# A sliding-window attention's value products regrouped: one run of sixteen for a pair of heads instead of two of twelve

## What is computed

```python
s = jnp.einsum('bnqhgd,bnjhd->bhgnqj', q, kb).astype(jnp.float32)   # banded: 3 key blocks of 128 for a query block
s = jnp.where(mask, s + bias, lowest)
m = jnp.maximum(jnp.max(s, axis=-1, keepdims=True), sink)
p = jnp.exp(s - m)
p = p / (jnp.sum(p, axis=-1, keepdims=True) + jnp.exp(sink - m))
o = jnp.einsum('bhgnqj,bnjhd->bnqhgd', p.astype(v.dtype), vb).reshape(B, S, D)
return jnp.einsum('bsd,de->bse', o, w_o)
```

## Time and profile before

| | before |
|---|---|
| time, median of 3 executions | 1100.08 us (1099.56 to 1100.72) |
| the profiled execution | 1099.98 us, span 1098.3 us |
| tensor engine busy | 1085.3 us, 99% of the span |
| weight loads busy | 957.7 us, 87% |
| vector engine busy | 879.1 us, 80% |
| scalar engine busy | 597.8 us, 54% |
| granted clock of the tensor engine | 0.998 |

### The profile page before, as it was taken

The page is one execution under the profiler, slowest core; times in us unless marked ns, Lnnn a source line. Parts: engine busy times, 40 slices in busy tenths (PEclk is TensorE's granted clock), DMA queues, the critical chain, the costliest instruction groups (busy, mean ns, idle before and its releaser), DMA issues. The chain is left out here.

```text
span 1098.3 us, 18147 instructions
## 1 busy us (share of the span) xinstructions
PE 1085.3 (99%) x6526; PEld 957.7 (87%) x6526; DVE 879.1 (80%) x1523; ACT 597.8 (54%) x1025; POOL 142.6 (13%) x252
## 2 busy tenths in 40 slices
PE   8999999999999999999999999999999999999997
PEld 6888888888998898898997888888899899899896
DVE  7777888678877876886996799976895895985997
ACT  6777777655425434433554788854542542632544
POOL 6554332100000000000030244200000000000000
PEclk9999999999999999999999999999999999999999
DMA  5422332233323323323242133334313323223312
GB/s 206 124 86 88 90 99 61 84 97 142 116 81 104 104 81 113 99 89 121 78 126 76 54 97 90 88 106 134 101 74 124 91 93 116 96 96 116 118 56 77
DMA packets 37081, 109.64 MB, mean 100 GB/s; under 512 B 6464, under 2 KB 10848, under 8 KB 37008
## 3 DMA queue, kind: packets, MB, share of 16 engines
q1 hardware_dynamic: 32096, 100.74, 27.9%
q0 software_dynamic: 4768, 7.90, 3.0%
q10 hardware_dynamic: 144, 0.02, 0.0%
HBM read 105.93 MB, written 2.70 MB: 99 GB/s over the span
## 5 line engine op out<-in xcount | busy, mean ns | idle before, releaser
L639 PE MATMUL acc<-h_hi,w_parts 128*128 128x512 f32 x736 | 291.0, 395 | 2.6 <-DVE h_lo L1590 1.6
L641 PE MATMUL acc<-h_hi,w_parts 128*128 128x512 f32 x736 | 286.8, 390 | 0.0
L640 PE MATMUL acc<-h_lo,w_parts 128*128 128x512 f32 x736 | 286.6, 389 | 0.0
L639 PEld LDWEIGHTS acc<-h_hi,w_parts 128*128 128x128 f32 x736 | 138.2, 188 | 32.8 <-issue 3.0
L641 PEld LDWEIGHTS acc<-h_hi,w_parts 128*128 128x128 f32 x736 | 138.2, 188 | 29.5
L640 PEld LDWEIGHTS acc<-h_lo,w_parts 128*128 128x128 f32 x736 | 138.3, 188 | 27.8 <-issue 0.5
L1272 ACT CAST w_parts<-w_raw 128x1024 fp32r<-128x1024 f32 x62 | 65.4, 1054 | 131.7 <-PE acc L641 107.5
L639 PE MATMUL pt_ps<-u_hi,w_parts 128*128 128x256 f32 x384 | 109.2, 284 | 0.3 <-DVE x_res L1815 0.2
L640 PE MATMUL pt_ps<-u_lo,w_parts 128*128 128x256 f32 x384 | 108.7, 283 | 0.0
L641 PE MATMUL pt_ps<-u_hi,w_parts 128*128 128x256 f32 x384 | 108.7, 283 | 0.0
L639 PE MATMUL s_ps<-u_hi,w_parts 128*128 128x256 f32 (+1 forms) x292 | 86.5, 296 | 0.0
(11 more groups left out here) (208 smaller groups left out, 2491.2 us busy)
## 6 DMA issues: line engine op xcount, KB each, us to landing
w_raw<-in_wstream SPq DMA_DIRECT2D x148, 512.0 KB, 3.6
d_raw<-in_wstream SPq DMA_DIRECT2D x32, 512.0 KB, 5.2
room<-rpb_reversed POOLq DMA_DIRECT2D x64, 62.0 KB, 2.5
room<-t_shifted POOLq DMA_DIRECT2D x64, 48.0 KB, 2.2
x_res<-in_xT SPq DMA_DIRECT2D x8, 256.0 KB, 6.1
room<-inverse_sums SPq DMA_DIRECT2D x16, 128.0 KB, 3.1
out_y<-x_res SPq DMA_DIRECT2D x8, 256.0 KB, 2.3
inverse_sums<-sw_turned SPq DMA_DIRECT2D x32, 1.0 KB
```

The lines of the kernel that those rows point to most:

```text
L639: nc.tensor.matmul(dst, a[0], b[0], start=start, stop=False, skip_group_check=resumed)
L640: nc.tensor.matmul(dst, a[0], b[1], start=False, stop=False, skip_group_check=resumed)
L641: return nc.tensor.matmul(dst, a[1], b[0], start=False, stop=stop, skip_group_check=resumed)
```

## The change

The turned probabilities get a new layout. The high parts of a pair lie in one room and the low parts in the other. In each the ten combinations of key block and unit stand in the order of the blocks, and within a block in the order of the units, so that all units that see a block are neighbours. A head gets a bank of om_ps for itself, all four query blocks in it. The value products of a pair are now one run: for each head key block 0 (units 0 and 1, 256 columns), block 3 (units 2 and 3, 256 columns), block 1 (units 0 to 2, 384 columns) and block 2 (units 1 to 3, 384 columns), each with the high and the low part, sixteen products with the same 5120 columns in all. The run of the pair before stands between dense_part(1) and the transposes of unit 0. The two old places are empty. After the last step the whole run of the last pair stands where its second group did. sw_o_shift and sw_o_sum read the new banks, and the count of pv_done goes up once a pair instead of twice.

```diff
-        sw_pt = [t.rearrange("p (t b h u q) -> p t b h u q", t=2, b=3, h=2, u=2)
-                 for t in (flat(pt_room),)]
-        sw_pt.insert(0, w_parts[:, 0, :, 2 * CHUNK:].rearrange("p t (b h u q) -> p t b h u q", b=3, h=2, u=2))
+        sw_pt = [w_parts[:, 0, :, 2 * CHUNK:2 * CHUNK + 10 * P].rearrange("p h (c q) -> p c h q", q=P),
+                 flat(pt_room)[:, 0:20 * P].rearrange("p (h c q) -> p c h q", h=2, q=P)]
...
-        sw_near = om_ps[:].rearrange("p g (h u) q -> p g h (u q)", h=2)
+        sw_near = om_ps[:].rearrange("p h n q -> p h (n q)")
...
             first, blocks = SW_BLOCKS[n]
-            first -= n // 2
-            return sw_pt[n // 2][:, t, first:first + blocks, :, n % 2, :].rearrange("p b h q -> p (b h) q")
+            at = 2 * first + n
+            return sw_pt[t][:, at:at + 2 * blocks - 1:2, :, :]
...
-            def sw_values(p, g):
-
-                pe.wait_ge(pt_split, (sw_unit(p, 2 * g + 1) + 1).v)
+            def sw_values(p):
+
+                pe.wait_ge(pt_split, (sw_unit(p, 3) + 1).v)
                 pe.wait_ge(o_summed, (p + HEADS).v)
-                dst = flat(sw_bank(g)).rearrange("p (h u q) -> p h u q", h=2, u=2)
-                both, only = ((0, 1), 2) if g == 0 else ((1, 2), 0)
-
-                def products(hh, b, units, start=False, stop=False):
-                    stationary = flat(v_parts[:, 4 * p.odd + g + b, hh, :, :])
-                    for t in range(2):
-                        ins = nc.tensor.matmul(dst[:, hh, units, :], stationary, sw_pt[g][:, t, b, hh, units, :],
-                                               start=start and t == 0, stop=stop and t == 1)
-                    return ins
-
                 for hh in range(2):
-                    products(hh, both[0], slice(0, 2), start=hh == 0)
-                    products(hh, both[1], slice(0, 2))
-                for hh in range(2):
-                    ins = products(hh, only, slice(1 - g, 2 - g), stop=hh == 1)
+                    for b in (0, 3, 1, 2):
+                        units = [n for n in range(QT) if SW_BLOCKS[n][0] <= b < sum(SW_BLOCKS[n])]
+                        at, count = 2 * b + units[0], len(units)
+                        for t in range(2):
+                            ins = nc.tensor.matmul(om_ps[:, hh, units[0]:units[0] + count, :], flat(v_parts[:, 4 * p.odd + b, hh, :, :]),
+                                                   sw_pt[t][:, at:at + count, hh, :], start=b == 0 and t == 0,
+                                                   stop=b == 2 and t == 1)
                 ins.then_inc(pv_done, 1)
...
                 dense_part(1)
+                if before:
+                    sw_values(p + -1)
                 sw_transpose(p, 0)
-                if before:
-                    sw_values(p + -1, 1)
                 sw_scores(p, 2)
...
                 sw_transpose(p, 2)
-                sw_values(p, 0)
                 dense_part(6)
...
             early_part(CH_SWO, GR_SWO, HEADS, 14, 17)
-            sw_values(At(7), 1)
+            sw_values(At(7))
...
-                act.wait_ge(pv_done, (p * 2 + (UNITS_NA + 2)).v)
+                act.wait_ge(pv_done, (p + (UNITS_NA + 1)).v)
                 act.wait_ge(o_summed, (p + HEADS).v)
-                nc.scalar.copy(by_group(sw_far)[TOP, :, :], sw_near[BOTTOM, :, 0, :])
-                nc.scalar.copy(by_group(sw_far)[BOTTOM, :, :], sw_near[TOP, :, 1, :]).then_inc(o_shifted, 1)
+                nc.scalar.copy(sw_far[TOP, :], sw_near[BOTTOM, 0, :])
+                nc.scalar.copy(sw_far[BOTTOM, :], sw_near[TOP, 1, :]).then_inc(o_shifted, 1)
```

More of the change, by code:

```diff
@@ L378, in sw_pt_part, with by_block @@
             first, blocks = SW_BLOCKS[n]
-            first -= n // 2
-            return sw_pt[n // 2][:, t, first:first + blocks, :, n % 2, :].rearrange("p b h q -> p (b h) q")
-        def sw_bank(g):
-            return misc_ps if g else o_ps
+            at = 2 * first + n
+            return sw_pt[t][:, at:at + 2 * blocks - 1:2, :, :]
+        def by_block(n):
+            return pt_ps[:, 0:2 * SW_BLOCKS[n][1], :].rearrange("p (b h) q -> p b h q", h=2)
         def sw_unit(p, n):
@@ L1395, in sw_pt_high @@
                 act.wait_ge(pt_done, (sw_unit(p, n) + 1).v)
-                nc.scalar.copy(sw_pt_part(0, n), pt_ps[:, 0:2 * SW_BLOCKS[n][1], :]).then_inc(pt_hi_made, 1)
+                nc.scalar.copy(sw_pt_part(0, n), by_block(n)).then_inc(pt_hi_made, 1)
             def sw_o_shift(p):
-                act.wait_ge(pv_done, (p * 2 + (UNITS_NA + 2)).v)
+                act.wait_ge(pv_done, (p + (UNITS_NA + 1)).v)
                 act.wait_ge(o_summed, (p + HEADS).v)
-                nc.scalar.copy(by_group(sw_far)[TOP, :, :], sw_near[BOTTOM, :, 0, :])
-                nc.scalar.copy(by_group(sw_far)[BOTTOM, :, :], sw_near[TOP, :, 1, :]).then_inc(o_shifted, 1)
+                nc.scalar.copy(sw_far[TOP, :], sw_near[BOTTOM, 0, :])
+                nc.scalar.copy(sw_far[BOTTOM, :], sw_near[TOP, 1, :]).then_inc(o_shifted, 1)
             def sw_o_high(p):
@@ L1994, in sw_pt_low @@
                 dve.wait_ge(pt_hi_made, (sw_unit(p, n) + 1).v)
-                nc.vector.tensor_tensor(sw_pt_part(1, n), pt_ps[:, 0:2 * SW_BLOCKS[n][1], :], f32(sw_pt_part(0, n)),
+                nc.vector.tensor_tensor(sw_pt_part(1, n), by_block(n), f32(sw_pt_part(0, n)),
                                         ALU.subtract).then_inc(pt_split, 1)
             def sw_o_sum(p):
-                dve.wait_ge(pv_done, (p * 2 + (UNITS_NA + 2)).v)
+                dve.wait_ge(pv_done, (p + (UNITS_NA + 1)).v)
                 dve.wait_ge(o_shifted, (p + (UNITS_NA + 1)).v)
@@ L2004, in sw_o_sum @@
                     rows = HEAD_ROWS[hh]
-                    ins = nc.vector.tensor_tensor(by_group(sw_o)[rows, :, :], sw_near[rows, :, hh, :],
-                                                  by_group(sw_far)[rows, :, :], ALU.add)
+                    ins = nc.vector.tensor_tensor(sw_o[rows, :], sw_near[rows, hh, :], sw_far[rows, :], ALU.add)
                 ins.then_inc(o_summed, 1)
```

## The result

| | before | after |
|---|---|---|
| time, median of 4 executions each | 1100.40 us (1099.56 to 1101.90) | 1111.48 us (1110.97 to 1112.89) |
| ratio, with its 95% interval | | 1.0101 (1.0089 to 1.0113) |
| the profiled execution | 1099.98 us, span 1098.3 us | 1112.89 us, span 1109.6 us |
| tensor, weight loads, vector, scalar busy | 1085.3, 957.7, 879.1, 597.8 us | 1086.8, 954.5, 879.6, 598.4 us |

The change costs 1% of the program, 9.8 to 12.4 us. The whole program's busy times don't show it: no engine's moves by more than 3.2 us. The time went into waits. The spans compare more cleanly than the times here: the profiled execution of after spends 3.3 us outside its span, the three others of after 1.7 to 2.0 with spans of 1109.3 to 1109.7.

A forecast was written before the change was run, and what follows sets the result against it. It took the vector engine to bound each step, the tensor engine just behind. Six steps +8.8 us, first step -0.8, last step +0.5 and tail +1.0 make 9.5, added to 1099.98: 1109.5 us, range 1105.0 to 1113.5.

The forecast's parts named there:

- (e): Second attention's steps: the forecast itself, the walk as it stands, 1109.5 us; chance 0.65.
- the walk through the step: One steady step followed across tensor, vector and scalar engine queues: 1.52 us late, step of 14.60 us.
- T3: Transposes of unit 3 on the tensor engine, start of a step; forecast to recur after 14.60 us instead of 13.08.
- T0: Transposes of unit 0 on the tensor engine, queued behind the run; forecast to start at 5.20 us instead of 2.83.
- T1: Transposes of unit 1 on the tensor engine, gated by the low part of unit 0; forecast at 7.28 us.
- The layout at zero: Copies into the new layout, shifts and sums of outputs: no cost, 0.3 us a step at the utmost.
- What the removed products are worth: A pair's value products, 24 to 16: 2.37 us against 2.88, saving 0.51 a pair, but lying in a wait.
- (d): Value run: matmul time goes by columns, so the merged run takes 2.88 us; 1113.6 us, chance 0.07.
- (a): Second attention: removed instructions decide, tensor engine is the bound, vector engine catches up; 4.1 us go, 1095.9 us, chance 0.08.
- (c): Each step: vector engine's free 0.57 us absorbs part of the wait, about 1.0 us lost; 1106.7 us, chance 0.12.
- (b): Whole program: gain and new wait cancel, nothing to be measured; 1100 us, chance 0.05.
- First step, last step and last run: Ends of the second attention: first step 0.77 us gained, last step 0.5 lost, last value run (tail) 1.02 lost.

The follow-up runs named there:

- later sinks: Kernel before with only the two sink exponentials moved behind the high part of unit 3 on the scalar engine: 1100.09 us, ratio 1.0000.
- the version by key blocks: After, run cut: blocks 1, 0 ahead of T0, blocks 3, 2 behind; eighteen products, dense products redistributed, sink exponentials later: 1100.43 us, 1.0006.
- the four with the heads apart: After with mirrored rooms, head 0 ahead of T0, head 1 behind T0 or unit 2's scores: 1104.57, 1106.01 us; with sink exponentials later: 1103.85, 1105.32.
- the two with other orders of the copies: Shifts behind unit 1's high part, sums and scaling behind unit 3's logits, sink exponentials late: 1110.77 us with halved run, 1108.75 with before's products and places.

## Why the prediction was right

The forecast was 1109.5 us in a range of 1105.0 to 1113.5; 1111.48 was measured. The mechanism was the forecast one (e), and the walk through the step held item by item. The times in after, from T3, come from the rows above, the forecast ones from the prediction:

| | forecast | measured |
|---|---|---|
| length of the run of sixteen | 2.37 | 2.37 |
| T0 | 5.20 | 5.15 |
| low part of unit 0 | 6.45 | 6.40 |
| T1 | 7.28 | 7.24 |
| high part of unit 1 | 8.21 | 8.20 |
| low part of unit 1 | 9.05 | 9.03 |
| next T3 | 14.60 | 14.58 |

- **What bounds the kernel.** Right in what the forecast used, that the vector engine has no time to give once T0 is late: of a run ahead of T0 all but 0.8 us is paid in full, at three lengths. As a whole the picture was too simple. A step of before goes through both engines, the tensor engine from T3 to the scores of unit 2 and the vector engine from there to the next T3. The later sinks show the one side (a wait less on the vector engine, the same time), the version by key blocks the other (less work for the tensor engine behind those scores, the same time). The forecast didn't depend on it, since with the run ahead of T0 no wait for those scores is left.
- **The layout at zero.** Right. The high copies of 512 and 768 columns still take 0.59 and 0.80 us, the low parts 0.69 and 0.95 to 0.96, the shifts 0.58, and the version by key blocks has this layout at before's time.
- **What the removed products are worth.** Right against the two old runs where they stood (1.44 us each), too high for the merging itself, and harmless, since the term stood in a wait. I took 0.12 us for a short product from a run of twelve right behind transposes; in a row of twenty-four ahead of them it is 0.115, and merging saves 0.39 us a pair. The rival (d), that the columns decide (a run of 2.88), is refuted by the run of 2.37 us. The page that I had set against this term ("TensorE: Matmul & The Clock Gate", Back-to-back issue gap, in the Trainium skill: about 81 ns for a pair of 128 columns) is not borne out here, with 115.
- **The rival (a)**, the removed instructions decide, is refuted by the time, by the vector engine's idle time of 1.40 us, and by the old products in after's place, which do the old work and lose 1.92 us a step. **(c)**, part of the wait absorbed by the free 0.57 us, falls with a loss of 1.51 us a step where it had 1.0; the vector engine's small waits are still there (0.30 us ahead of the low part of unit 3, 0.26 ahead of that of unit 1). **(b)** falls with the ratio's interval.
- **The terms of the sum.** First step, last step and last run came out within 0.1 us of their terms. The last step's value I had put in the middle of two bounds (-0.5 and +1.5); it hit, but nothing in the rows had made it likelier than its neighbours.
- **Where the 2 us above the forecast are.** The spans differ by 11.3 us, 1.8 more than forecast; the other 0.2 lies outside them. Three places of the accounting had no term. The first T0 is 0.71 us late; nothing of the change lies before it, and in the traces of the kernels of this study it comes at anything from 612.95 to 614.25. The delay is there, whole, after 20 us of the span (see the clock, below), and in before and after nothing is added in the 593.6 us from there to T0. So it belongs to the two profiled executions and not to the change. The last run waits 0.26 us longer. I had found 0.56 us to spare for it in a steady step and not looked at the last, where fewer dense products stand ahead of it. And 0.37 us lies in the 380 us behind, unexplained.
- **One misplaced detail.** I had put the tensor engine's own wait of a microsecond before T3. It is there, but one item earlier, before the scores of unit 0 of the next pair (0.94, for the queries' low part), with 0.22 left before T3. Before T1 it is 0.33, where I had said about half a microsecond.

My guesses for the versions were worse than for the change. Six of the twelve runs missed: the four with the heads apart and the two with other orders of the copies. Each time I had named what was late after the repair of one wait and stopped there, while the next item of some queue was a few tenths behind it. The version by key blocks, in which T0, the scores of unit 2 and the shifts all keep their old times, came out at the slow end of what I had expected (steps of 12.8 to 13.1, measured 13.10 on average): it gave back the loss, and the gain from the shorter wait for unit 3 didn't come, for the reason that the later sinks had shown.

## What to carry to other kernels

Where an engine that feeds on another's small products (here: turned probabilities) has next to no gap, the place of a lump of work on the feeding engine decides, not its length in sum: all of a lump ahead of the feeding product beyond the slack (0.8 us here) is paid in every step. Fewer instructions on the feeding engine bring nothing if they are saved where it isn't awaited: a step can be bound by a way through both engines, and only what lies on it counts. Before merging two runs into one, walk one step through all queues from the spot where the merged run must stand, and then walk on to the item that is late next, since it is the second or third that decides. Keep the merged form, and cut it where the queue has room: that cost nothing here, and gained nothing.

## What the runs showed of the hardware

**Who shares with the vector engine.** A subtraction or multiplication of 512 columns with both inputs in SBUF takes 0.69 us on the vector engine. The scaling takes 1.59 to 1.62 in the two reordered kernels, in each step where GpSimd's subtraction of 1.28 us starts some 0.2 us before it, and 1.49 in the one step where it starts 0.34 before. Even before the change such a pair met in the first step (0.69 us elsewhere):

```profile
619.17 1.28 POOL L573 TENSOR_TENSOR u_hi<-room,u_hi 64x512 fp32r<-64x512 f32 x1 [11.50 <-issue]
...
619.70 1.29 DVE L2034 TENSOR_TENSOR u_lo<-room,u_lo 64x512 fp32r<-64x512 f32 x1 [0.47 <-ACT u_lo L1141]
```

In these pairs the vector engine's instruction ends about 0.55 us after GpSimd's: at 620.99 against 620.45 (619.17 + 1.28), and at 664.25 against 663.69. That is most of its own 0.69, as if it had hardly run before (the profile's spans on GpSimd are rough). The logits, which read one of their inputs from PSUM, keep their 0.48 us beside it (in before at 645.75, with GpSimd's subtraction from 645.23 to 646.51). The Trainium skill, "SBUF — State Buffer", Who interferes with whom, says that GpSimd shares a pair of SBUF ports with the vector engine and that only this pair is contended for; the trace agrees.

**What a short product costs.** With 32-bit rounded operands and new weights for each product, 128 columns cost as much as 256: 24 products, 16 of them of 256 and 8 of 128, take 2.76 us, 0.115 each, and scores of 256 columns alone follow each other at 0.12. A product of 384 columns costs 0.17 to 0.18. So merging pays for pieces of 128 columns alone.

**Clock.** At the program's start, the tensor engine is idle for 1.98 us in after and for 1.64 in before, and the granted clock behind it is lower in after. The timeline of the tensor engine and the windows (columns as in the first view above, the clock third from the end) of after:

```profile
8.53 0.77 PE L638 MATMUL acc<-h_hi,w_parts 128*128 128x512 f32 x1 [1.98 <-DVE h_lo L1581]
```

```profile
5.00:10.00 5.00, 3.02 (x11) 2.16 (x10) 2.86 (x3) 4.27 (x7) 1.57 (x2) 0.85 1.04 381
10.00:15.00 5.00, 5.00 (x19) 3.58 (x18) 4.78 (x7) 4.20 (x9) 1.38 (x3) 0.81 0.89 313
```

And of before:

```profile
8.30 0.48 PE L639 MATMUL acc<-h_hi,w_parts 128*128 128x512 f32 x1 [1.64 <-DVE h_lo L1590]
```

```profile
5.00:10.00 5.00, 3.29 (x13) 2.04 (x11) 3.42 (x4) 4.72 (x8) 1.41 (x2) 1.00 1.02 375
```

So the profiled execution of after spent part of these ten microseconds at the lower of the two levels (1.2 instead of 2.4 GHz), and before did not; of the fourteen traces after's is the only one that did. Its products from 8.53 on start 0.43 us apart, those of before 0.23. Waits of up to 0.94 us in the middle of the second attention left the clock at 1.00.

The late first T0 comes from this start. The first product is 0.23 us later than in before (8.53, 8.30), the first one of the next chunk 0.67 (11.39, 10.72), the sums for the norm 0.72, and T0 0.71. Of the sums, after and before:

```profile
20.62 1.00 PE L713 MATMUL om_ps<-ones,sqsum 128*128 128x1 f32 x8
```

```profile
19.90 1.05 PE L714 MATMUL om_ps<-ones,sqsum 128*128 128x1 f32 x8
```

What of it is the clock and what the later start, no run took apart. The other executions of after have no trace; their spans are within 0.4 us of each other, and the granted clock over the whole execution (0.996 to 0.998) does not order them.
